# Output product of the token mixers in split one-pass products, with its weights split in eight pieces between the attention units

## The chip, the cores and the metric

The kernel runs on one core of one Trainium2 chip. The metric is the device time of one execution in microseconds, as the median of three runs. The engines meant below: TensorE (PE in the rows; PEld are its weight loads), VectorE (DVE), ScalarE (ACT), SyncE, which issues most transfers (SP).

## What is computed

A decoder trunk of two layers on 256 tokens of width 1024, in float32. Each layer adds a token mixer and then a channel mixer (dense in layer 0, top 2 of 8 experts in layer 1). The change is in the last line of the token mixer:

```python
def token_mixer(h, w_in, ..., w_out):
    proj = h @ w_in
    ...
    o_a = nsa_mixer(q, k_c, v_c, k_s, v_s, k_w, v_w, gl, cmp_pe, cmp_w1, cmp_w2)   # 512 columns
    o_b = conformer_conv(conv_in, conv_w, conv_b, conv_ln_g, conv_ln_b, conv_pw)   # 256 columns
    o_c = retention(rq, rk, rv, rg, ret_gn)                                        # 256 columns
    return jnp.concatenate([o_a, o_b, o_c], axis=-1) @ w_out                       # (256, 1024) @ (1024, 1024)

for l in range(DEPTH):
    h = rmsnorm(x, ln_attn[l])
    x = x + token_mixer(h, w_in[l], ..., w_out[l])
    h = rmsnorm(x, ln_ffn[l])
    x = x + (swiglu(h, ...) if l % 2 == 0 else moe_ffn(h, ...))
```

## The kernel before

**Two kinds of product.** A product of float32 tiles (`mm` on F32) is shown in the trace as two matmul records. The second kind, `three`, splits both operands beforehand in a rounded part (type F32R) and the remainder, and adds three one-pass matmuls: rounded by rounded, rounded by remainder, remainder by rounded. The input projections and the channel mixers are made in the second way: ACT copies a piece of the weights from the ring into its rounded part (`whM`, `whU`, `whD`), DVE subtracts that from the ring for the remainder (`ringl`, `wlU`, `wlD`). The output product and the small products of the attention are of the first kind.

**The output product.** The concatenated heads stand turned in `catT`, eight chunks of 128 channels by 256 tokens. Chunks 4 and 5 come from the convolution (stage `conv_pw`), 6 and 7 from the retention (`retcat`), 0 to 3 from the attention (`attn_sum` 0 and 1, by token tile). The output is four tiles of 128 tokens by 512 columns, k = 2 i + h for token tile i and column half h, each in a PSUM bank of its own. Stage `out` k makes the four products of chunks 4 to 7, and `out_rest` k those of chunks 0 to 3. I call such four products a group. The weights of half h are one item of the ring (`WO + h`).

**The order of the work.** Nothing schedules: `MIXER` is a list of stages written out by hand, and every engine walks it and does its own part of each stage, in order, with waits on semaphores. The attention is 12 units. Unit k has `probT` k (TensorE turns the exponentials, ACT copies them out), then what `AHEAD` names, `score` k+2 (TensorE; DVE takes the maximum; ACT the exponentials), then what `BESIDE` names for k, then `pv` k (TensorE; DVE scales it out of PSUM). `BESIDE` holds the pieces of the other mixers (`hid`, `cnorm`, `retnorm`, `cscore`, `cpv`, `out`) and `TAIL` what follows the last unit, up to the addition of the result to `x` (DVE) and its turned copy (`xT`), which the channel mixer reads. `pre` 0 and 1 split the first weights of the channel mixer.

**Banks.** PSUM groups take eight banks in turn; from the first `out` on, four banks are kept for the output and the others turn over four. A group waits until the one that held its bank before is evicted.

Of the kernel before, what the change touches and what calls it, by code (L numbers as in the profile page):

```python
# [15 lines left out]
P = 128  # L16
D = 1024
T = 256
# [58 lines left out]
def conv(a, b):  # L77
# [16 lines left out]
          3: [("reto", 0), ("hid", 0), ("cnorm", 0)], 4: [("croot", 0), ("hid", 1), ("retnorm", 0)], 5: [("cnorm", 1)],  # L94
          6: [("retnorm", 1)], 7: [("cmpkv", 0), ("conv_pw", 0)],
# [4 lines left out]
TAIL = [("osum", 1), ("pre", 0), ("out_rest", 0), ("attn_sum", 1), ("pre", 1), ("out_rest", 1), ("out_rest", 2), ("xT", 0),  # L100
        ("xT", 1), ("out_rest", 3), ("xT", 2), ("xT", 3)]
# [52 lines left out]
VW, RET, CONV, QK, W1K, W1VN, WO = range(7)  # L154
LAST_READ = (None, ("rqk", 1, 0), ("kcv", 0, 0), ("ks", 0, 0), ("cmpkv", 0, 0), ("cmpkv", 0, 0),
# [105 lines left out]
def hybrid_trunk_kernel(nc, x_in, consts_in, params_in, mix_in, ffn_in, moe_in, router_in, final_in, out):  # L261
    with ExitStack() as ctx:
# [3 lines left out]
        def sem(name):  # L266
            return ctx.enter_context(nc.semaphore(name))
# [52 lines left out]
        ro = mix("ro", [P, NT, RET_HEADS, HD])  # L320
        gates = mix("gates", [P, NT, HEADS, 3])
# [22 lines left out]
        cacc = mix("cacc", [P, 2, NC, T])  # L344
# [54 lines left out]
        whM = [nc.alloc_sbuf_tensor_at(f"whM{h}", [P, KD, FC], F32R, offset=home_at[h]) for h in range(4)]  # L399
        beforeb = sb("beforeb", [P, P], BF16)  # L400
# [77 lines left out]
        s_rk = sem("s_rk")  # L478
        s_conv_in = [sem(f"s_conv_in{h}") for h in range(2)]
# [179 lines left out]
        def _(pe):  # L659
# [81 lines left out]
            def mixer(l):  # L741
                for stage, k in MIXER[l]:
# [210 lines left out]
                    elif stage == "retcat":  # L953
                        o = begin(l, stage)
                        pe.wait_ge(s_ret, l + 1)
                        for m in range(2):
                            for i in range(NT):
                                q = m * NT + i
                                last = flip(o[:, q * P:(q + 1) * P],
                                            ro[:, i, 2 * m:2 * m + 2, :].rearrange("p h d -> p (h d)"))  # L960
                        is_full(last, l, stage)
                    elif stage == "out":
                        i, h = divmod(k, 2)
                        o = begin(l, stage, k)
# [3 lines left out]
                        landed(l, WO + h)  # L968
                        w = weights(l, WO + h, 512)
                        for c in range(KD // 2, KD):  # L970
                            mm(o, catT[:, c, i * P:(i + 1) * P], w[:, c, :], c == KD // 2, False)
                    elif stage == "out_rest":
                        i, h = divmod(k, 2)
                        w = weights(l, WO + h, 512)
# [216 lines left out]
        def _(act):  # L1191
# [40 lines left out]
            def mixer(l):  # L1232
                for stage, k in MIXER[l]:
# [110 lines left out]
                    elif stage == "attn_sum":  # L1344
                        full(act, l, stage, k)
                        is_free(A(catT[:, 0:4, k * P:(k + 1) * P],
                                  bank(l, stage, k).rearrange("p (q t) -> p q t", q=4), ACT.Copy), l, stage, k)
                    elif stage in ("conv_pw", "retcat"):
                        full(act, l, stage)
                        m = 4 if stage == "conv_pw" else 6  # L1350
                        is_free(A(catT[:, m:m + 2, :], bank(l, stage).rearrange("p (q t) -> p q t", q=2), ACT.Copy),
                                l, stage)
# [220 lines left out]
        def _(dve):  # L1573
# [64 lines left out]
            def mixer(l):  # L1638
                for stage, k in MIXER[l]:
# [627 lines left out]
```

## Time and profile before

| | us |
|---|---|
| median of three runs | 1275.2 (1274.94 to 1275.55) |
| the profiled execution | 1274.92, its span 1272.9 |
| TensorE busy | 1253.7 (98%) |
| DVE busy | 996.8 (78%) |
| ACT busy | 856.6 (67%) |
| granted TensorE clock, mean | 0.997 of 2.4 GHz |

The span is what the trace covers, so all places in it are given in us from its start. Layer 0's token mixer ends near 158 us, layer 1's near 493; the experts take the rest. A busy share is a mean over stages: an engine at 67% can still be the one that is waited for at a given place.

### The profile page before, as it was taken

Reading aid. Unit: us, or ns where it says so; the run is one execution under the profiler, and the core shown is the slowest. Engines: PE = TensorE matmul, PEld = TensorE weight load, DVE = VectorE, ACT = ScalarE, POOL = GpSimd, SP = SyncE. Lnnn points to the kernel's source line nnn. Section 1 sums busy time; section 2 is a strip of 40 time slices with the busy share of each in tenths; the row PEclk is TensorE's granted clock in tenths of the full one; section 3 lists DMA queues with packets and bytes.
Section 4 is the critical chain, followed back from the end, with each engine's and each line's share of the span. In section 5 each row is a group of like instructions: output and inputs, shape, how many; then the busy total and the mean of one; then the engine's idle time right before and its main releaser. Section 6 shows DMA issues by size and latency. Waiting matters only on the chain.

```text
span 1272.9 us, 16264 instructions
## 1 busy us (share of the span) xinstructions
PE 1253.7 (98%) x6313; PEld 1015.9 (80%) x6313; DVE 996.8 (78%) x1110; ACT 856.6 (67%) x1225; POOL 31.0 (2%) x21
## 2 busy tenths in 40 slices
PE   9999999999999999999999999999999999999996
PEld 8797588888779866788888888888888888888885
DVE  4886455455569646998999989889889889889997
ACT  4335264444451544978878888878878878878885
POOL 0000000000000000010000000000000000000300
PEclk9999999999999999999999999999999999999999
DMA  9433194442521336899999999999999999999991
GB/s 370 165 143 133 71 388 175 174 184 103 198 100 71 143 132 267 340 401 372 394 369 372 390 380 374 386 371 383 389 369 381 389 372 358 396 373 351 415 370 39
DMA packets 38625, 367.62 MB, mean 289 GB/s; under 512 B 4112, under 2 KB 7312, under 8 KB 11152
## 3 DMA queue, kind: packets, MB, share of 16 engines
q1 hardware_dynamic: 35808, 356.56, 71.2%
q0 software_dynamic: 1440, 5.24, 1.1%
q10 hardware_dynamic: 1296, 4.72, 0.9%
q8 instruction: 53, 0.87, 0.3%
q14 instruction: 28, 0.23, 0.0%
HBM read 360.73 MB, written 5.77 MB: 288 GB/s over the span
## 4 chain that ended last, share of the span: by engine, by line
PE 92%; DVE 4%; ACT 2%; issue 0%; DMA 0%; DVEq 0%; ACTq 0%
PE ps L661 88%; PE ps L664 4%; ACT arena L1294 1%; DVE blocks L1674 1%; DVE wlU L1856 1%; DVE arena L1692 0%; DVE wlD L1863 0%; ACT arena L1304 0%; DMA x<-x_in 0%; ACT xn L1196 0%; ACT L1286 0%; ACT L1341 0%; DVE arena L1765 0%; DVE xn L1596 0%; DVE ringl L1635 0%
## 5 line engine op out<-in xcount | busy, mean ns | idle before, releaser
L1856 DVE TENSOR_TENSOR wlU<-ring,whU 128x2048 fp32r<-128x2048 f32 x196 | 448.8, 2290 | 57.6 <-ACT whU L1386 53.1
L1386 ACT ACTIVATE whU<-ring 128x1024 fp32r<-128x1024 f32 x396 | 417.6, 1060 | 60.8 <-PE ps L661 53.2
L661 PE MATMUL ps<-whU,hTh 128*128 128x512 f32 x880 | 352.7, 401 | 0.8 <-DVE wlU L1856 0.8
L661 PE MATMUL ps<-whU,hTl 128*128 128x512 f32 x880 | 345.0, 392 | 0.0
L661 PE MATMUL ps<-wlU,hTh 128*128 128x512 f32 x880 | 343.0, 390 | 0.0
L1863 DVE TENSOR_TENSOR wlD<-ring,whD 128x2048 fp32r<-128x2048 f32 x97 | 222.1, 2290 | 39.2 <-ACT whD L1398 39.0
L1398 ACT ACTIVATE whD<-ring 128x1024 fp32r<-128x1024 f32 x194 | 205.2, 1066 | 58.9 <-PE ps L661 52.7
L661 PEld LDWEIGHTS ps<-whU,hTl 128*128 128x128 f32 x880 | 165.1, 188 | 36.1
L661 PEld LDWEIGHTS ps<-wlU,hTh 128*128 128x128 f32 x880 | 166.0, 189 | 32.4
L661 PEld LDWEIGHTS ps<-whU,hTh 128*128 128x128 f32 x880 | 165.3, 188 | 32.7 <-DVE wlU L1856 1.0
L661 PE MATMUL ps<-whD,gTh 128*128 128x512 f32 x428 | 168.6, 394 | 0.5 <-DVE gTl L1881 0.5
L661 PE MATMUL ps<-whD,gTl 128*128 128x512 f32 x428 | 167.4, 391 | 0.0
L661 PE MATMUL ps<-wlD,gTh 128*128 128x512 f32 x428 | 166.6, 389 | 0.0
L661 PEld LDWEIGHTS ps<-whD,gTh 128*128 128x128 f32 x428 | 80.4, 188 | 19.7 <-DVE wlD L1863 3.6
L661 PEld LDWEIGHTS ps<-wlD,gTh 128*128 128x128 f32 x428 | 80.7, 189 | 16.4
L661 PEld LDWEIGHTS ps<-whD,gTl 128*128 128x128 f32 x428 | 80.3, 188 | 16.9
L1412 ACT ACTIVATE gTh<-ps 128x256 fp32r<-128x256 f32 x107 | 40.3, 386 | 54.6 <-PE ps L664 54.6
L661 PEld LDWEIGHTS ps<-arena 128*128 128x128 f32 (+1 forms) x472 | 56.6, 190 | 14.5 <-issue 12.7
L661 PE MATMUL ps<-arena 128*128 128x64 f32 (+6 forms) x472 | 65.2, 297 | 2.3 <-ACT arena L1304 2.3
L1881 DVE TENSOR_TENSOR gTl<-ps,gTh 128x256 fp32r<-128x256 f32 x107 | 44.2, 421 | 27.5 <-ACT gTh L1412 27.5
L664 PE MATMUL ps<-cst,arena 128*128 128x128 f32 x376 | 63.3, 273 | 1.2 <-DVE arena L1802 1.1
L664 PEld LDWEIGHTS ps<-cst,arena 128*128 128x128 f32 x376 | 48.2, 143 | 17.2 <-issue 3.6
(232 smaller groups left out, 1224.7 us busy)
## 6 DMA issues: line engine op xcount, KB each, us to landing
ring<-moe_in SPq DMA_DIRECT2D x88, 2048.0 KB, 8.4
ring<-moe_in SPq DMA_DIRECT2D x88, 1024.0 KB, 8.6
ring<-ffn_in SPq DMA_DIRECT2D x11, 2048.0 KB, 7.6
ring<-mix_in SPq DMA_DIRECT2D x5, 3072.0 KB, 10.8
ring<-ffn_in SPq DMA_DIRECT2D x11, 1024.0 KB, 6.9
ring<-mix_in SPq DMA_DIRECT2D x4, 2048.0 KB, 10.5
ring<-mix_in SPq DMA_DIRECT2D x2, 2176.0 KB, 8.6
ring<-mix_in SPq DMA_DIRECT2D x2, 2112.0 KB, 8.1
```

Source lines behind the costliest of these rows:

```text
L661: return nc.tensor.matmul(o, lhsT, rhs, start=first, stop=last, skip_group_check=True)
L664: return nc.tensor.transpose(o, a, ident)
L1294: last = A(prob[:, k % 3, c * keys:(c + 1) * keys], bank(l, stage, k)[:, c * keys:(c + 1) * keys], ACT.Exp, bias=nmax[:, k, c:c + 1], scal ...
L1386: A(whU[:, p, :], ring[:, f.slot(J), p * PIECE:(p + 1) * PIECE], ACT.Copy).then_inc(s_hi, 1)
L1398: A(wh_down(f, J, c), ring[:, f.slot(J), (UP + c) * PIECE:(UP + c + 1) * PIECE], ACT.Copy)\
L1412: A(g_high(f, J, i), ps[:, up_bank(f, J, i), 0:FC].rearrange("p (c t) -> p c t", c=DOWN), ACT.Copy)\
L1674: last = V.tensor_tensor(blocks[lo:lo + HD, v, hi, :, g, 0:NBLK], src[g * HD:(g + 1) * HD, v, :, hi:hi + NBLK, r], spread(pe_[lo:lo + HD, ...
L1856: V.tensor_tensor(wlU[:, w, :], raw, whU[:, w, :].bitcast(F32), ALU.subtract).then_inc(s_lo, 1)
L1863: V.tensor_tensor(wl_down(f, J), raw, high.bitcast(F32), ALU.subtract).then_inc(s_lo, 1)
L1881: V.tensor_tensor(g_low(f, J, i), ps[:, up_bank(f, J, i), 0:FC].rearrange("p (c t) -> p c t", c=DOWN), g_high(f, J, i).bitcast(F32), ALU.s ...
```

## The change

The output product goes over to the second kind. Per layer:
- A new stage `wo` q, eight per layer: ACT copies two chunks of 512 columns of the weights (128x1024) into `woh`, DVE subtracts for the remainder in `ringl`. They stand at units 4, 5, 7, 8, 9, 10, 11 and at the head of `TAIL`.
- The heads are evicted twice: ACT writes the rounded part `cath`, then DVE reads the same bank and writes the remainder `catl`. The bank comes free after DVE.
- The groups call `out_row`, three one-pass matmuls for each chunk, and wait for their pieces of the weights.
- The groups stand elsewhere: `out` 0 at unit 8, `out` 2 at unit 9, none at unit 10, `out` 1 at unit 11, `out` 3 in `TAIL`. Before they were at 8, 9, 10 and 11.
- Some tiles are laid elsewhere in memory so that the new ones fit.

```diff
-          8: [("cscore", 0), ("out", 0)], 9: [("out", 1)],
-          10: [("cprobT", 0), ("out", 2), ("cpv", 0), ("cpv", 1)],
-          11: [("out", 3), ("asum", 0), ("asum", 1), ("osum", 0), ("attn_sum", 0)]}
+          8: [("cscore", 0), ("out", 0), ("wo", 3)], 9: [("out", 2), ("wo", 4)],
+          10: [("cprobT", 0), ("wo", 5), ("cpv", 0), ("cpv", 1)],
+          11: [("out", 1), ("wo", 6), ("asum", 0), ("asum", 1), ("osum", 0), ("attn_sum", 0)]}
...
+WO_ROWS = ((0, 4), (0, 6), (0, 0), (0, 2), (1, 4), (1, 6), (1, 0), (1, 2))
...
+            def out_row(l, o, i, h, c, first, final):
+
+                if c % 2 == 0:
+                    pe.wait_ge(s_wol, len(WO_ROWS) * l + WO_ROWS.index((h, c)) + 1)
+                t = slice(i * P, (i + 1) * P)
+                low = ringl[:, mix_load(l, WO + h) % SLOTS, 512 * c:512 * (c + 1)]
+                return three(o, cath[:, c, t], catl[c // 2][:, c % 2, t], woh[l][2 * h + (c < 4)][:, c % 4, :], low, first, final)
...
                     elif stage == "out_rest":
                         i, h = divmod(k, 2)
-                        w = weights(l, WO + h, 512)
                         freed(pe, l, "attn_sum", i)
                         for c in range(KD // 2):
-                            last = mm(bank(l, "out", k), catT[:, c, i * P:(i + 1) * P], w[:, c, :], False,
-                                      c == KD // 2 - 1)
+                            last = out_row(l, bank(l, "out", k), i, h, c, False, c == KD // 2 - 1)
...
+                    elif stage == "wo":
+                        h, c = WO_ROWS[k]
+                        n = mix_load(l, WO + h)
+                        act.wait_ge(slot_full[n % SLOTS], filled(n))
+                        if k == 0:
+                            full(act, l, "kcv")
+                        elif k == 6:
+                            full(act, l, "retcat")
+                        A(wo_high(l, k), wo_rows(ring, l, k), ACT.Copy).then_inc(s_woh, 1)
...
+                    elif stage == "wo":
+                        dve.wait_ge(s_woh, len(WO_ROWS) * l + k + 1)
+                        V.tensor_tensor(wo_rows(ringl, l, k), wo_rows(ring, l, k), wo_high(l, k).bitcast(F32), ALU.subtract)\
+                            .then_inc(s_wol, 1)
+                    elif stage in ("conv_pw", "retcat"):
+                        m = 4 if stage == "conv_pw" else 6
+                        dve.wait_ge(s_cath, CATS * l + (m == 6) + 1)
+                        is_free(V.tensor_tensor(catl[m // 2][:], bank(l, stage).rearrange("p (q t) -> p q t", q=2),
+                                                cath[:, m:m + 2, :].bitcast(F32), ALU.subtract), l, stage)
```

ACT's list in units 4 to 6, before: the copy of `hid` 1 (L1307), the copy of `probT` 5 (L1304), the exponentials of score 7 (L1294), the copy of `probT` 6, then the activation of `convB` (L1341) with its table load.

```order
L1307 ACTIVATE arena<-ps 128x256
L1304 ACTIVATE arena<-ps 128x512
L1294 ACTIVATE arena<-ps,arena 128x256 x2
L1304 ACTIVATE arena<-ps 128x512
L1341 ACT_TABLE_LOAD
L1341 ACTIVATE arena<-ps,par 128x256 x2
```

The same place of the changed kernel, whose lines stand some 27 further down:

```order
L1334 ACTIVATE arena<-ps 128x256
L1388 ACTIVATE woh_74<-ring 128x1024
L1331 ACTIVATE arena<-ps 128x512
L1321 ACTIVATE arena<-ps,arena 128x256 x2
L1388 ACTIVATE woh_74<-ring 128x1024
L1331 ACTIVATE arena<-ps 128x512
L1368 ACT_TABLE_LOAD
L1368 ACTIVATE arena<-ps,par 128x256 x2
```

The two pieces (L1388) stand right ahead of the copies of `probT` 5 and 6.

DVE's list in units 7 and 8, before: the two evictions of `cmpkv`, the three instructions of `pv` 7, the maximum of score 10, and the start of `cscore` (L1737).

```order
L1727 COPY arena<-ps 128x32
L1728 TENSOR_TENSOR arena<-ps,cst 128x512
L1699 RECIPROCAL arena<-arena 128x2
L1703 TENSOR_TENSOR arena<-arena 128x2
L1706 TENSOR_TENSOR arena<-ps,arena 128x128
L1692 TENSOR_REDUCE arena<-ps 128x2
L1694 TENSOR_SCALAR arena<-arena 128x2
L1737 SCALAR_TENSOR_TENSOR arena<-ps,cst 128x64 x4
```

And in the changed kernel, where L1848 makes the remainder of two chunks of heads and L1843 that of a weight piece:

```order
L1764 COPY arena<-ps 128x32
L1765 TENSOR_TENSOR arena<-ps,cst 128x512
L1848 TENSOR_TENSOR catl_85<-ps,cath 128x512
L1843 TENSOR_TENSOR ringl<-ring,woh_75 128x1024
L1736 RECIPROCAL arena<-arena 128x2
L1740 TENSOR_TENSOR arena<-arena 128x2
L1743 TENSOR_TENSOR arena<-ps,arena 128x128
L1848 TENSOR_TENSOR catl_86<-ps,cath 128x512
L1729 TENSOR_REDUCE arena<-ps 128x2
L1731 TENSOR_SCALAR arena<-arena 128x2
L1774 SCALAR_TENSOR_TENSOR arena<-ps,cst 128x64 x4
```

Two remainders of heads (of `conv_pw` and `retcat`) and one of weights come in ahead of the maximum of score 10.

DVE's list in units 10 and 11, before: `pv` 9 and `pv` 10 (three instructions each), then `asum` 0 and 1 (L1808) and `osum` 0 (L1812).

```order
L1699 RECIPROCAL arena<-arena 128x4
L1703 TENSOR_TENSOR arena<-arena 128x4
L1706 TENSOR_TENSOR arena<-ps,arena 128x256
L1699 RECIPROCAL arena<-arena 128x2
L1703 TENSOR_TENSOR arena<-arena 128x2
L1706 TENSOR_TENSOR arena<-ps,arena 128x128
L1808 TENSOR_TENSOR arena<-arena 128x512 x2
L1812 TENSOR_TENSOR arena<-arena 128x512
```

And in the changed kernel:

```order
L1843 TENSOR_TENSOR ringl<-ring,woh_76 128x1024
L1736 RECIPROCAL arena<-arena 128x4
L1740 TENSOR_TENSOR arena<-arena 128x4
L1743 TENSOR_TENSOR arena<-ps,arena 128x256
L1843 TENSOR_TENSOR ringl<-ring,woh_76 128x1024
L1736 RECIPROCAL arena<-arena 128x2
L1740 TENSOR_TENSOR arena<-arena 128x2
L1743 TENSOR_TENSOR arena<-ps,arena 128x128
L1843 TENSOR_TENSOR ringl<-ring,woh_77 128x1024
L1861 TENSOR_TENSOR arena<-arena 128x512 x2
L1865 TENSOR_TENSOR arena<-arena 128x512
L1854 TENSOR_TENSOR catl_83<-ps,cath 128x2x128
```

The remainders of pieces 4, 5 and 6 stand ahead of `pv` 9, `pv` 10 and the sums.

## Rows read from the trace of the kernel before

**Rows 1.** The page, its first line and the busy line of TensorE.

```profile
span 1272.9 us, 16264 instructions
PE 1253.7 (98%) x6313; PEld 1015.9 (80%) x6313; DVE 996.8 (78%) x1110; ACT 856.6 (67%) x1225; POOL 31.0 (2%) x21
```

**Rows 2.** Windows: stretch, length; busy of PE, PEld, DVE, ACT, POOL; granted clock; DMA.

```profile
98.67:158.02 59.35, 57.63 (x327) 38.16 (x326) 32.34 (x77) 26.35 (x66) 0.00 (x0) 1.00 0.27 103
434.17:493.52 59.35, 57.83 (x328) 38.36 (x328) 31.40 (x77) 29.29 (x75) 0.00 (x0) 1.00 0.27 102
```

**Rows 3.** Timeline of TensorE, layer 0: start, length, instruction, count, idle before.

```profile
106.61 0.63 PE L664 MATMUL ps<-cst,arena 128*128 128x128 f32 x4 [0.53 <-DVE arena L1802]
...
114.52 1.08 PE L661 MATMUL ps<-arena 128*128 128x64 f32 x8 [0.48 <-ACT arena L1304]
...
119.28 3.70 PE L661 MATMUL ps<-ring,arena 128*128 128x512 f32 x8
...
125.07 3.60 PE L661 MATMUL ps<-ring,arena 128*128 128x512 f32 x8
128.50 1.00 PE L661 MATMUL ps<-arena 128*128 128x64 f32 x8
...
133.44 2.72 PE L661 MATMUL ps<-arena 128*128 128x512 f32 x12
...
139.87 0.60 PE L664 MATMUL ps<-cst,arena 128*128 128x128 f32 x4
...
141.16 3.70 PE L661 MATMUL ps<-ring,arena 128*128 128x512 f32 x8
...
157.62 0.63 PE L664 MATMUL ps<-cst,x 128*128 128x128 f32 x4 [0.71 <-DVE x L1820]
```

**Rows 4.** Timeline of TensorE, channel mixer: first and last of 62 matmuls.

```profile
160.17 0.39 PE L661 MATMUL ps<-whU,hTh 128*128 128x512 f32 x1
...
174.05 0.39 PE L661 MATMUL ps<-wlU,hTh 128*128 128x512 f32 x1
```

**Rows 5.** Two copies in a row (timeline), then groups by line and form.

```profile
141.00 1.99 ACT L1386 ACTIVATE whU<-ring 128x1024 fp32r<-128x1024 f32 x2
...
L1386 ACT ACTIVATE whU<-ring 128x1024 fp32r<-128x1024 f32 x396 | 417.6, 1060 | 60.8 <-PE ps L661 53.2 <-ACT ystage L1488 3.2
...
L1849 DVE TENSOR_TENSOR wlU<-ring,whU 128x1024 fp32r<-128x1024 f32 x4 | 4.8, 1223 | 4.5 <-ACT whU L1386 4.5
```

**Rows 6.** Timeline of ACT, layer 0, units 4 to 7.

```profile
103.32 0.37 ACT L1307 ACTIVATE arena<-ps 128x256 f32<-128x256 f32 x1
103.82 0.60 ACT L1304 ACTIVATE arena<-ps 128x512 f32<-128x512 f32 x1
...
107.10 0.60 ACT L1304 ACTIVATE arena<-ps 128x512 f32<-128x512 f32 x1 [0.17 <-ACT arena L1294]
...
113.78 0.60 ACT L1304 ACTIVATE arena<-ps 128x512 f32<-128x512 f32 x1 [0.17 <-ACT arena L1294]
...
117.35 0.60 ACT L1351 ACTIVATE arena<-ps 128x512 f32<-128x512 f32 x1
```

**Rows 7.** Timeline of DVE, layer 0: end of retnorm 0, and the tail.

```profile
104.32 0.17 DVE L1776 TENSOR_SCALAR arena<-arena 128x8 f32<-128x8 f32 x1
...
152.20 0.69 DVE L1820 TENSOR_TENSOR x<-ps,x 128x512 f32<-128x512 f32 x1 [1.46 <-PE ps L661]
...
157.38 0.68 DVE L1828 TENSOR_TENSOR hT<-ps,par 128x512 f32<-128x512 f32 x1
```

**Rows 8.** Timeline of SP: the issue of the second weight half; issues with median landing.

```profile
112.28 0.33 SPq L587 DMA_DIRECT2D ring<-mix_in  x1
...
ring<-mix_in SPq DMA_DIRECT2D x4, 2048.0 KB, 10.5
```

**Rows 9.** Windows of 2 us in the router, columns as in rows 2.

```profile
498.00:500.00 2.00, 2.00 (x15) 1.28 (x14) 1.86 (x11) 0.03 (x1) 0.00 (x0) 0.50 1.05 451
500.00:502.00 2.00, 1.97 (x13) 1.41 (x12) 1.96 (x6) 1.47 (x2) 0.00 (x0) 0.78 0.90 385
```

More of the change, by code:

```diff
@@ L93 @@
 BESIDE = {0: [("rets", 0)], 1: [("rets", 1)], 2: [("convT", 0)],
-          3: [("reto", 0), ("hid", 0), ("cnorm", 0)], 4: [("croot", 0), ("hid", 1), ("retnorm", 0)], 5: [("cnorm", 1)],
-          6: [("retnorm", 1)], 7: [("cmpkv", 0), ("conv_pw", 0)],
-          8: [("cscore", 0), ("out", 0)], 9: [("out", 1)],
-          10: [("cprobT", 0), ("out", 2), ("cpv", 0), ("cpv", 1)],
-          11: [("out", 3), ("asum", 0), ("asum", 1), ("osum", 0), ("attn_sum", 0)]}
-TAIL = [("osum", 1), ("pre", 0), ("out_rest", 0), ("attn_sum", 1), ("pre", 1), ("out_rest", 1), ("out_rest", 2), ("xT", 0),
-        ("xT", 1), ("out_rest", 3), ("xT", 2), ("xT", 3)]
+          3: [("reto", 0), ("hid", 0), ("cnorm", 0)], 4: [("croot", 0), ("hid", 1), ("retnorm", 0), ("wo", 0)],
+          5: [("cnorm", 1), ("wo", 1)], 6: [("retnorm", 1)], 7: [("cmpkv", 0), ("conv_pw", 0), ("wo", 2)],
+          8: [("cscore", 0), ("out", 0), ("wo", 3)], 9: [("out", 2), ("wo", 4)],
+          10: [("cprobT", 0), ("wo", 5), ("cpv", 0), ("cpv", 1)],
+          11: [("out", 1), ("wo", 6), ("asum", 0), ("asum", 1), ("osum", 0), ("attn_sum", 0)]}
+TAIL = [("wo", 7), ("osum", 1), ("out", 3), ("pre", 0), ("out_rest", 0), ("attn_sum", 1), ("pre", 1), ("out_rest", 1),
+        ("out_rest", 2), ("xT", 0), ("xT", 1), ("out_rest", 3), ("xT", 2), ("xT", 3)]
 MIXER = [OPEN[l] + HEAD + [z for k in range(len(UNITS))
@@ L320, in hybrid_trunk_kernel @@
         ro = mix("ro", [P, NT, RET_HEADS, HD])
+        cln = mix("cln", [P, NT, CONV_CH])
+        csq = mix("csq", [P, NT, CONV_CH])
+        cacc = mix("cacc", [P, 2, NC, T])
         gates = mix("gates", [P, NT, HEADS, 3])
@@ L399, in hybrid_trunk_kernel @@
         whM = [nc.alloc_sbuf_tensor_at(f"whM{h}", [P, KD, FC], F32R, offset=home_at[h]) for h in range(4)]
+        wo_at = (xn_at, hT_at, ring_at + 4 * 4096, arena_at + 4 * mix_at["rp0"])
+        woh = [[nc.alloc_sbuf_tensor_at(f"woh{l}{q}", [P, 4, 512], F32R,
+                                        offset=wo_at[q] + 4 * SLOT * (mix_load(l, WO + 1) % SLOTS) * (q == 2))
+                for q in range(4)] for l in range(DEPTH)]
+        cath = nc.alloc_sbuf_tensor_at("cath", [P, KD, T], F32R, offset=arena_at + 4 * mix_at["catT"])
+        catl = [nc.alloc_sbuf_tensor_at(f"catl{q}", [P, 2, T], F32R,
+                                        offset=arena_at + 4 * (mix_at["cln"], mix_at["csq"], mix_at["cacc"], mix_at["cacc"] + 512)[q])
+                for q in range(4)]
         beforeb = sb("beforeb", [P, P], BF16)
@@ L478, in hybrid_trunk_kernel @@
         s_rk = sem("s_rk")
+        s_woh = sem("s_woh")
+        s_wol = sem("s_wol")
+        s_cath = sem("s_cath")
         s_conv_in = [sem(f"s_conv_in{h}") for h in range(2)]
@@ L540, in piece_of, with wo_rows, wo_high @@
             return w[:, :, col:col + FC]
+        def wo_rows(buf, l, q):
+            h, c = WO_ROWS[q]
+            return buf[:, mix_load(l, WO + h) % SLOTS, 512 * c:512 * (c + 2)].rearrange("p (c n) -> p c n", c=2)
+        def wo_high(l, q):
+            h, c = WO_ROWS[q]
+            return woh[l][2 * h + (c < 4)][:, c % 4:c % 4 + 2, :]
         def half_of(i, h):
@@ L1345, in mixer @@
                         full(act, l, stage, k)
-                        is_free(A(catT[:, 0:4, k * P:(k + 1) * P],
-                                  bank(l, stage, k).rearrange("p (q t) -> p q t", q=4), ACT.Copy), l, stage, k)
+                        A(cath[:, 0:4, k * P:(k + 1) * P], bank(l, stage, k).rearrange("p (q t) -> p q t", q=4), ACT.Copy)\
+                            .then_inc(s_cath, 1)
                     elif stage in ("conv_pw", "retcat"):
@@ L1370, in mixer @@
                             act.wait_ge(s_root, NT * 3 + i + 1)
+                            full(act, l, "out", 2)
                             A(xh[:, i, :], x[:, i, :], ACT.Copy, scale=stat[:, 3, i:i + 1]).then_inc(s_xh, 1)
@@ L1803, in mixer @@
                             .then_inc(s_cln, 1)
+                    elif stage == "wo":
[7 more added lines that the diff above has]
+                                                cath[:, m:m + 2, :].bitcast(F32), ALU.subtract), l, stage)
+                    elif stage == "attn_sum":
+                        dve.wait_ge(s_cath, CATS * l + 2 + k + 1)
+                        t = slice(k * P, (k + 1) * P)
+                        for q in range(2):
+                            last = V.tensor_tensor(catl[q][:, :, t], bank(l, stage, k).rearrange("p (q t) -> p q t", q=4)
+                                                   [:, 2 * q:2 * q + 2, :], cath[:, 2 * q:2 * q + 2, t].bitcast(F32), ALU.subtract)
+                        is_free(last, l, stage, k)
                     elif stage == "asum":
```

12 lines of the change are left out of this document (4 added, 8 removed).

## The prediction, made before the changed kernel was run

> **What bounds the kernel now.** I read the page first. TensorE is busy for 1253.7 of 1272.9 us [rows 1], so only a wait that is added to its queue, or work that is taken out of it, moves the end. Then I cut out the two stretches that the change touches, from unit 4 of the attention to the first product of the channel mixer, one for each layer [rows 2]: 59.35 us each (98.67 to 158.02 and 434.17 to 493.52, 335.50 us apart), at granted clock 1.00 (2.4 GHz). TensorE works 57.6 of them, DVE 32.3, ACT 26.4. The timeline of TensorE names its only waits there: 0.53 us ahead of convB, 0.48 ahead of pv 7 and 0.71 ahead of the last xT [rows 3]. All my times are those of layer 0; layer 1 is taken as the same. DVE and ACT seem to have 27 and 33 us to spare per layer. But each runs its list in program order, so what counts is where an inserted instruction stands in that list and who waits for the one behind it.
>
> **What the change takes off TensorE.** One group of four products (half of a 128x512 tile) lasts 125.07 to 128.50, 3.43 us [rows 3]. In one-pass form it is 12 matmuls of 512 columns. Such matmuls run back to back in the first step of the channel mixer: 61 of them start between 160.17 and 174.05, one per 0.2275 us, and 12 take 2.73 us [rows 4]. So a group gains 0.70 us; with eight groups per layer that is 5.6 us, 11.2 us for both layers. A rule that promises more: the Trainium skill, page "TensorE: Matmul & The Clock Gate", section "Back-to-back issue gap", gives about 131 ns per matmul of 512 columns in a long stream. By it a group would take 1.57 us and the gain be 29.8 us. With the waits found below the time would be 1262.8. The trace disagrees, with 227.5 ns for this same form of instruction, so that rule gets no chance and I go by the trace.
>
> **What it adds elsewhere, per layer.** ACT gets eight copies 128x1024: two of them in a row take 1.99 us, one record is 1.06 [rows 5], so the next instruction can start 0.93 after one. DVE gets eight subtractions 128x1024, 1.22 us by the four records of that size [rows 5]; the next starts some 0.07 earlier, 1.15. DVE also gets the remainders of the heads: two of 128x512 (0.69 us by an addition of that size out of PSUM [rows 7], some 0.6 to the next) and two of twice 128x256 (0.7 by the same row). That is 7.4 us on ACT and 11.8 on DVE, less than both have idle. Handovers are read from the same rows: about 0.2 us from TensorE to ACT or DVE, 0.15 back and 0.04 between ACT and DVE (estimates from where a record starts against the end of the one it waits for). I walk the list in steps.
>
> **Step A, unit 4.** On ACT weight piece 0 follows the hid 1 copy (103.32, 0.37 long [rows 6]) and ends at 104.7. The copy of probT 5, at 103.82 before, waits for it until 104.55 and pv 5 on TensorE for that copy. DVE ended retnorm 0 at 104.4 [rows 7], waits for piece 0 and subtracts until 105.85, so pv 4, the maximum of score 7 and cnorm 1 come 1.4 us late. TensorE waits at convB until 108.0 instead of 106.61.
>
> **Step B, units 5 to 7.** The exponentials of score 7 are late by 1.4 and piece 1 stands behind them, so the copy of probT 6 moves from 107.10 to 109.5, 2.4 late. From 107.10 to the copy of probT 7 at 113.78 ACT has no pause over 0.2 us (two table loads, silu, two roots) [rows 6]. All of it moves by 2.35, and with it pv 7: 116.85 instead of 114.52. TensorE is now 2.35 us late.
>
> **Step C, units 7 and 8.** DVE's list here is conv_pw remainder, piece 2, pv 7, retcat remainder, maximum of score 10. The conv_pw copy of ACT comes at 119.7 (117.35 before [rows 6]), its remainder on DVE ends at 121.0, ACT ends piece 2 at 121.2, DVE its subtraction at 122.4, pv 7 (0.6) at 123.05, and the retcat remainder at 123.7. out 0 needs that remainder: it starts at 123.85, where TensorE was ready at 119.28 [rows 3] + 2.35 = 121.6, a wait of 2.2. It is 4.55 late now. out 0 and out 2 give 1.4 back: 3.15 late.
>
> **Step D, unit 10.** Before, a group stood between cprobT and cpv 0, which began at 133.44 [rows 3], and covered ACT's two copies. It is moved away, so cpv 0 waits for the copies of probT 10 and cprobT, 0.2 + 0.49 + 0.38 + 0.15 less the 0.2 of cprobT itself, 1.05, and cpv 1 some 0.2 more for DVE. At this point 3.43 has gone and 1.25 come: 1.0 late, with a group of 2.73 still owed.
>
> **Step E, unit 11.** out 1 ends at 140.1. ACT copies probT 11 at 137.7, then piece 6 until 139.2; DVE subtracts until 140.4 and only then does the sums asum 0, asum 1 (0.7 each) and osum 0 (0.69), until 142.4. attn_sum 0 starts at 142.55 instead of 139.87 [rows 3]: a wait of 2.4, and 2.7 late.
>
> **Step F, tail.** pv 11, the owed group, then out_rest 0 at 146.55 instead of 141.16, 5.4 late. Three groups give back 2.1; out_rest 2 ends 3.2 late. The fourth gains nothing: the last xT waits for an addition that DVE does after a chain of hT and hTl pieces. That chain starts with the addition of out_rest 2 (152.20, to 157.38, then xT at 157.62 [rows 3, 7]), so it moves by some 3.1 and the shorter out_rest 3 only waits longer.
>
> **Sum.** +3.1 us per layer, made of -5.6 from the products and +8.7 of waits. The channel mixer starts 3.1 later in layer 0 and runs as before. In layer 1 the router, which hangs on the same last product, moves with it. The profiled execution took 1274.92 us, the median of the three runs is 1275.2, 0.3 more; 6.2 on the median is 1281.4.
>
> **Bounds of the unknown.** No row has these subtractions in this place. If each were hidden better than I walk it, the two soft waits (2.2 in C and 2.4 in E) could halve: 2.3 per layer off, 1276.8. If each of the eight pieces costs 0.25 more in handover, it is 4 us over both layers, 1285.4. The second half of the weights is no limit: its transfer is issued at 112.28, lands some 10.5 us later [rows 8], and ACT first needs it at 132, so even 2 us later it is there.
>
> **The rivals.**
> *All hidden, faster.* The 19 us of new work per layer fall into 27 and 33 us of idle time and TensorE keeps its pace: 1275.2 - 11.2 = 1264.0. For it: those totals. Against: the idle time lies behind waits for TensorE, and steps A and B need no assumption but the order. Chance 0.04. *Half hidden:* only A, B and D bite, 3.6 per layer against 5.6: 1271.2. It decides if the retcat remainder and osum 0 come at least 2 us earlier than I have them. Chance 0.05.
> *A draw.* C and E at half, and the maximum of score 7 not held up: about 1275. Chance 0.07.
> *The clock falls too.* In the router the granted clock went to 0.50 and 0.78 in two slices of 2 us [rows 9]. That cost 1.4 us. If each of the four longer waits (C and E, twice) brought the like, it adds about 6: 1287. Against: 0.5 us waits left the clock at 1.00. Chance 0.06.
> *As walked*, 0.78.
>
> **How the numbers follow.** A measurement tells 0.2% (2.55 us) from no change. Faster is the two hidden cases, 0.09; the draw 0.07; slower the walk and the clock, 0.84. The range 1276.8 to 1286.0 holds the walk with both bounds; outside it lie the hidden cases, most of the draw and the full fall of the clock.
>
> **What the profile after would show.** Step A: TensorE waits at pv 5 for the ACT copy and about 1.5 us at convB for cnorm. B: pv 7 starts 2.3 late, ACT without pause before it. C: the first matmul of out 0 waits 2 us for DVE's retcat remainder. D: 1 us ahead of cpv 0. E: 2.4 us ahead of attn_sum 0, released by osum. Product groups of 2.73. Windows over the same stages of 62.5 us instead of 59.35. I am wrong if out 0 or attn_sum 0 start without a wait, if the one-pass matmuls run slower or faster than 0.2275, or if the later stages shift too.

## The result, and the profile after

The changed kernel takes 1289.46 us, the median of four runs (1288.19 to 1290.35). The kernel before took 1275.38 beside it. The ratio is 1.0104, 95% interval 1.0092 to 1.0116: slower, as forecast, but by 14.1 us where I had 6.2, and outside my range (1276.8 to 1286.0).

The page of the changed kernel, its first line and TensorE's busy line, as in [rows 1]:

```profile
span 1287.1 us, 16450 instructions
...
PE 1254.2 (97%) x6377; PEld 1035.6 (80%) x6377; DVE 1020.7 (79%) x1138; ACT 871.9 (68%) x1241; POOL 28.8 (2%) x21
```

The span is 14.2 us longer. TensorE's busy time is the same, though 16 groups should have given back 11.2: something gave that back again. The windows over the same stages as in [rows 2], from probT 4 to the channel mixer:

```profile
99.26:165.16 65.90, 59.10 (x358) 49.56 (x358) 44.33 (x91) 34.01 (x74) 0.00 (x0) 0.90 0.24 92
441.33:507.14 65.81, 56.53 (x358) 46.45 (x358) 43.38 (x91) 36.81 (x83) 0.00 (x0) 0.95 0.24 92
```

They last 65.90 and 65.81 us, 6.55 and 6.46 more than before, where I had said 62.5. And the granted clock, 1.00 in both before, is 0.90 and 0.95. The rest of the 14.2 lies outside: 0.6 us ahead of the first window (probT 4 starts at 99.26, not 98.67; in e9 below, whose code is the same up to there, it starts at 98.69, so this part wanders from one execution to the next), nothing in the dense layer between the windows, 0.6 after the second.

TensorE's timeline of layer 0, with the waits of steps A and C to F:

```profile
105.85 1.08 PE L684 MATMUL ps<-arena 128*128 128x64 f32 x8 [0.56 <-ACT arena L1331]
106.77 0.61 PE L687 MATMUL ps<-cst,arena 128*128 128x128 f32 x4
108.61 0.90 PE L687 MATMUL ps<-cst,arena 128*128 128x128 f32 x4 [1.24 <-DVE arena L1839]
...
115.22 0.60 PE L684 MATMUL ps<-causalb,identb 128*128 128x512 bf16 x1
...
124.33 0.47 PE L684 MATMUL ps<-woh,cath 128*128 128x512 f32 x1 [0.41 <-DVE catl L1848]
124.64 0.40 PE L684 MATMUL ps<-ringl,cath 128*128 128x512 f32 x1
...
126.96 0.40 PE L684 MATMUL ps<-woh,catl 128*128 128x512 f32 x1
...
134.79 2.79 PE L684 MATMUL ps<-arena 128*128 128x512 f32 x12 [0.90 <-ACT arena L1348]
...
143.14 1.09 PE L687 MATMUL ps<-cst,arena 128*128 128x128 f32 x4 [2.34 <-DVE arena L1865]
...
146.58 0.63 PE L684 MATMUL ps<-woh,catl 128*128 128x512 f32 x1
147.01 0.63 PE L684 MATMUL ps<-woh,cath 128*128 128x512 f32 x1
...
150.37 0.40 PE L684 MATMUL ps<-woh,cath 128*128 128x512 f32 x1
...
164.78 0.63 PE L687 MATMUL ps<-cst,x 128*128 128x128 f32 x4 [1.36 <-DVE x L1873]
```

Two things are to be compared, where the waits stand and how long the work takes. The waits stand where the walk put them. With the 0.60 that all is late, attn_sum 0 was to start at 143.15 and did at 143.14. But the lengths do not: four turns of 128x128 take 0.61 at 106.77 and 0.90 behind the wait at 108.61, and 1.09 at 143.14. One-pass matmuls follow each other every 0.232 us at 124.64 to 126.96 and every 0.43 at 146.58. The windows of 4 us at those places say why:

```profile
104.00:108.00 4.00, 2.81 (x20) 2.14 (x18) 3.66 (x10) 1.80 (x5) 0.00 (x0) 1.00 0.00 0
108.00:112.00 4.00, 3.39 (x16) 3.24 (x17) 2.22 (x5) 3.85 (x8) 0.00 (x0) 0.60 0.00 0
112.00:116.00 4.00, 4.00 (x20) 3.67 (x19) 1.95 (x5) 3.94 (x11) 0.00 (x0) 0.54 0.00 0
...
144.00:148.00 4.00, 4.00 (x16) 3.52 (x15) 3.04 (x8) 3.43 (x4) 0.00 (x0) 0.50 0.02 4
148.00:152.00 4.00, 4.00 (x16) 3.18 (x15) 2.17 (x1) 0.00 (x0) 0.00 (x0) 0.78 0.00 0
```

The clock is at its lower level (0.50, 1.2 of 2.4 GHz) behind two waits: the pair 0.56 and 1.24 ahead of convB, and 2.34 ahead of attn_sum 0. Layer 1 has the same waits, but keeps its clock at convB:

```profile
450.68 0.63 PE L687 MATMUL ps<-cst,arena 128*128 128x128 f32 x4 [1.24 <-DVE arena L1839]
...
466.40 0.47 PE L684 MATMUL ps<-woh,cath 128*128 128x512 f32 x1 [2.10 <-DVE catl L1848]
...
470.82 1.00 PE L684 MATMUL ps<-arena 128*128 128x64 f32 x8
...
486.76 0.63 PE L687 MATMUL ps<-cst,arena 128*128 128x128 f32 x4 [2.34 <-DVE arena L1865]
```

There it falls behind out 0's wait, so that its group takes 4.42 us (466.40 to 470.82) instead of the 2.7 of the walk, and again behind attn_sum 0.

**What each fall cost.** In layer 0 the stages from convB to score 9 take 6.61 us (108.61 to 115.22) instead of the 3.53 of e8's rows below, 3.1 more. Yet out 0 starts on time, at 124.33 (walk: 123.85 + 0.60). The delay took the place of waits: that of pv 7, which is 1.09 in e8 and gone here, and that of out 0, of which 0.41 is left. The second fall has no such wait behind it. attn_sum 0 to out_rest 0 takes 7.23 instead of the 4.0 of my walk: +3.2. In layer 1 the two falls cost 1.7 each. So my theory after the result: per layer the walk's 3.1, as predicted, and 3.2 to 3.4 of clock. The rival: the waits and transfers between engines are longer than walked, and the clock is a symptom of TensorE idling more.

### The profile page after: what moved, and what is told of

Its sections match the earlier page's. It is cut to its first block, busy times and chain, and to the rows that moved or that the text cites. A ratio compares the mean times of both kernels' runs of the same rounds, so it can differ in the third digit from the quotient of the medians.

```text
span 1287.1 us, 16450 instructions
## 1 busy us (share of the span) xinstructions
PE 1254.2 (97%) x6377; PEld 1035.6 (80%) x6377; DVE 1020.7 (79%) x1138; ACT 871.9 (68%) x1241; POOL 28.8 (2%) x21
## 4 chain that ended last, share of the span: by engine, by line
PE 89%; DVE 6%; ACT 3%; issue 1%; DMA 0%; DVEq 0%; SPq 0%; ACTq 0%
PE ps L684 86%; PE ps L687 3%; ACT arena L1321 1%; DVE wlU L1909 1%; DVE blocks L1711 1%; DVE arena L1729 1%; ACT woh L1388 0%; DMA par<-params_in 0%; DVE ringl L1843 0%; DVE wlD L1916 0%; ACT arena L1331 0%; DVE x L1873 0%; ACT whU L1423 0%; DVE arena L1743 0%; DVE arena L1861 0%
## 5 line engine op out<-in xcount | busy, mean ns | idle before, releaser
L684 PE MATMUL ps<-arena 128*128 128x64 f32 (+6 forms) x472 | 68.3, 305 | 5.3 <-ACT arena L1331 3.5
L684 PEld LDWEIGHTS ps<-arena 128*128 128x128 f32 (+1 forms) x472 | 59.3, 198 | 15.8 <-issue 12.7
```

Of the source, the lines that this page charges most:

```text
L684: return nc.tensor.matmul(o, lhsT, rhs, start=first, stop=last, skip_group_check=True)
```

## The experiments

All ratios are to the kernel before, run beside each on the same chip (its medians: 1275.4 to 1276.3).

**e1 and e5: hold the clock, change nothing else.** `keep_busy(o, n)` issues n matmuls on constants of 128x256 (fillers), whose result the next product overwrites; the kernel before has it too, in other places, the router among them. In e1 they stand ahead of four waits, at convB (10) and out 0 (14), shown here, and likewise at pv 7 (8) and attn_sum 0 (18):

```diff
                     elif stage == "convB":
                         o = begin(l, stage)
+                        keep_busy(o, 10)
                         pe.wait_ge(s_cln, l + 1)
...
                         o = begin(l, stage, k)
                         if k == 0:
+                            keep_busy(o, 14)
                             freed(pe, l, "retcat")
```

> The changed kernel with empty bf16 matmuls (128x256, into the bank that is about to be written) put ahead of four of TensorE's waits in each layer: 10 ahead of the wait of convB, 8 ahead of pv 7, 14 ahead of out 0, 18 ahead of attn_sum 0. They only fill time in which TensorE waited. Theory (the clock): the waits themselves cost 6.3 us by my walk, the rest of the 14.1 us is the granted clock that falls behind them, so with the waits filled the clock stays at 1.00 there and the time is 1281 to 1283. Rival (the waits and the slower work are all from the other engines being late): filling changes nothing, 1289, or more, as the fillers delay. The granted clock of the stretches 98 to 166 us tells it apart.

Measured: 1288.05 us (1286.69 to 1288.29), ratio 1.0086 [1.0069, 1.0102]. Neither theory's time. The falls at convB and attn_sum 0 are gone, but at out 0 the clock fell in both layers (0.57 at 124 to 128 us, 0.71 at 464 to 468). The trace shows a flaw of mine: out 0's bank is the one that DVE evicts with the retcat remainder, so `begin` itself waits and the fillers stood behind the wait (2.06 us, released by L1854), adding 2.4 and 2.8 us to it. So e1 decides nothing for that place; e5 puts 16 fillers there, into the bank of `pv` 8, the stage that follows, which is free by then:

```diff
                         i, h = divmod(k, 2)
+                        if k == 0:
+                            keep_busy(begin(l, "pv", 8), 16)
                         o = begin(l, stage, k)
```

> The first filler kernel again with the fillers of out 0 in another place: in it they stood behind the wait for the bank of retcat, so they did not fill the wait of 2.06 us but followed it, 2.7 us long. Here 16 of them write into the bank of pv 8 ahead of that wait; the others stay (10 at convB, 8 at pv 7, 18 at attn_sum 0). Theory (the clock is what the walk lacked): granted clock 1.00 in all of both mixers, time 1282 (1281 to 1284). Rival (something else costs 8 us): 1287 or more with the clock at 1.00.

Measured: 1283.38 us (1282.84 to 1283.74), ratio 1.0059 [1.0044, 1.0075]. The windows over the same stages of e5:

```profile
98.81:161.52 62.71, 59.08 (x410) 48.79 (x410) 44.30 (x91) 34.02 (x74) 0.00 (x0) 1.00 0.26 97
437.81:500.43 62.62, 59.37 (x411) 48.88 (x410) 43.30 (x91) 36.82 (x83) 0.00 (x0) 1.00 0.25 96
```

With the clock at 1.00 the windows are 62.71 and 62.62: the 62.5 of the prediction. DVE and ACT do what they did in the changed kernel. This separates the two parts: some 6 us of the 14.1 are the clock (1289.46 to 1283.38), and the walk of waits and products is right to 0.2 us per layer. TensorE at `out` 0 and behind `out` 2 in e5:

```profile
123.88 0.47 PE L684 MATMUL ps<-woh,cath 128*128 128x512 f32 x1 [0.25 <-DVE catl L1854]
...
131.78 1.00 PE L684 MATMUL ps<-arena 128*128 128x64 f32 x8
```

The fillers delay nothing: `out` 0 starts 25.07 us after probT 4 (98.81 to 123.88), as it does in the changed kernel (99.26 to 124.33). The rival would have left windows of 65.8.

**e9 and e10: one fall at a time.** e9 keeps only the 18 fillers at attn_sum 0, e10 only those at convB (10) and pv 7 (8).

> The changed kernel with one addition: 18 matmuls on constants, whose result nobody reads, ahead of attn_sum 0 in both layers, in the 2.34 us in which TensorE waits there for osum. All else is as in the changed kernel. Theory (the clock's fall behind this wait is paid in full, because no later wait takes it up): attn_sum 0 to out_rest 0 is 3.2 us shorter in layer 0 and 1.7 in layer 1, so 4.9 in all, 1284.6 us; the granted clock is 1.00 from 140 to 152 us, and still falls behind convB in layer 0 and at out 0 in layer 1. Rival (the fall belongs to the stretch, not to the wait, and comes a little later all the same): 1288 to 1290, with the clock down somewhere between 145 and 160.

> The changed kernel with fillers only at its early waits: 10 matmuls on constants ahead of convB and 8 ahead of pv 7, in both layers. Theory (a fall ahead of out 0 is taken up by out 0's wait on the retcat remainder, since DVE sets when that comes): in layer 0 the clock stays at 1.00 from 104 to 120 us, TensorE comes to out 0 some 3 us earlier and waits there some 2 us instead of 0.41, and out 0's first product starts within 0.3 us of where it did. Nothing is gained: 1289, and up to 1291 if the clock then falls behind that longer wait, as it does in layer 1. Rival (each fall costs what it takes away, wherever it is): 3.1 less, 1286.3.

e9: 1286.34 us (1285.15 to 1287.94), ratio 1.0081 [1.0068, 1.0095], 3.1 faster than the changed kernel, not 4.9. e10: 1289.68 (1289.55 to 1290.58), ratio 1.011 [1.0095, 1.0126]: nothing gained, as its theory said. TensorE in e10:

```profile
106.90 1.26 PE L684 MATMUL ps<-warm 128*128 128x256 bf16 x10
108.22 0.66 PE L687 MATMUL ps<-cst,arena 128*128 128x128 f32 x4
...
124.04 0.47 PE L684 MATMUL ps<-woh,cath 128*128 128x512 f32 x1 [2.11 <-DVE catl L1850]
...
125.25 0.63 PE L684 MATMUL ps<-ringl,cath 128*128 128x512 f32 x1
```

The early fall is gone, and TensorE waits 2.11 at out 0 instead of 0.41. `out` 0 starts 25.10 us after probT 4 (98.94 to 124.04), as against 25.07 in the changed kernel: the early fall cost nothing at this point. Then the clock falls behind that longer wait, and out 0's group takes 4.42. That the whole window comes out the same as well (98.94 to 164.90, 65.96 us, as against 65.90) is in part luck: the fall behind attn_sum 0 was shorter here (5.72 us from attn_sum 0 to out_rest 0, as against 7.23) and gave back what out 0 had lost. So a fall ahead of a wait for another engine is free, and taking it away can bring on the next one. e9 shows the other half:

```profile
108.05 0.63 PE L687 MATMUL ps<-cst,arena 128*128 128x128 f32 x4 [1.24 <-DVE arena L1841]
...
123.77 0.77 PE L684 MATMUL ps<-woh,cath 128*128 128x512 f32 x1 [2.10 <-DVE catl L1850]
124.33 0.63 PE L684 MATMUL ps<-ringl,cath 128*128 128x512 f32 x1
...
141.58 2.14 PE L684 MATMUL ps<-warm 128*128 128x256 bf16 x18
143.99 0.66 PE L687 MATMUL ps<-cst,arena 128*128 128x128 f32 x4 [0.27 <-DVE arena L1867]
```

The fall behind attn_sum 0 is gone. But in layer 0 convB, with the same 1.24 us wait and the same work ahead, kept its clock this time (0.63, not 0.90), and out 0 lost it. That is the miss of 1.7: my expectation took the other falls as fixed. The same code has the fall now behind one wait, now behind the next, and the loss at one place is now 1.6, now 3.1.

**e8: pieces 0 and 1 alone, in the kernel before.** It tests steps A and B without the rest.

```diff
-          4: [("croot", 0), ("hid", 1), ("retnorm", 0)], 5: [("cnorm", 1)],
+          4: [("croot", 0), ("hid", 1), ("retnorm", 0), ("wo", 0)], 5: [("cnorm", 1), ("wo", 1)],
```

> The kernel before with only two of the eight weight pieces split at units 4 and 5, where the change has its first two; nothing reads them, products and order stay. It tests steps A and B alone. Theory: convB 1.4 us late, pv 7 2.35 late, and no later place gives it back, as in my walk: 2.35 per layer, 1281.0 with the clock at 1.00, and if the clock falls behind convB's wait, as in the changed kernel in layer 0, 1 to 4 more, up to 1285. Rival (the later idle time takes it in): 1277.

Measured: 1281.46 us (1279.61 to 1281.67), ratio 1.0039 [1.0023, 1.0054]. Two of eight pieces, with none of the products changed, cost 5 to 6 us (2.9 to 6.9 by the interval). TensorE in e8:

```profile
105.59 1.08 PE L664 MATMUL ps<-arena 128*128 128x64 f32 x8 [0.56 <-ACT arena L1307]
...
108.35 0.63 PE L667 MATMUL ps<-cst,arena 128*128 128x128 f32 x4 [1.24 <-DVE arena L1812]
...
111.88 0.38 PE L664 MATMUL ps<-causalb,identb 128*128 128x512 bf16 x1
...
117.15 1.08 PE L664 MATMUL ps<-arena 128*128 128x64 f32 x8 [1.09 <-ACT arena L1307]
```

With 0.33 us that e8 is late at its first window, pv 7 is 2.3 late against [rows 3]: step B's 2.35. The waits are those of the changed kernel to the hundredth, and the clock stayed at 1.00.

**e3: the order alone.** The kernel before with only the new places of the groups.

```diff
-          8: [("cscore", 0), ("out", 0)], 9: [("out", 1)],
-          10: [("cprobT", 0), ("out", 2), ("cpv", 0), ("cpv", 1)],
-          11: [("out", 3), ("asum", 0),
+          8: [("cscore", 0), ("out", 0)], 9: [("out", 2)],
+          10: [("cprobT", 0), ("cpv", 0), ("cpv", 1)],
+          11: [("out", 1), ("asum", 0),
```

> The kernel before with only the new places of the groups (out 0 at unit 8, out 2 at unit 9, none at unit 10, out 1 at unit 11, out 3 after the last unit), its product and weights untouched. Theory: only cpv 0 loses its cover, a wait of 1.0 us per layer, minus nothing: 1277.2, and the clock stays at 1.00 as no wait is over 1.1 us. Rival (the moved groups alone let the clock fall or start later waits): 1280 or more.

Measured: 1278.19 us (1277.28 to 1279.32), ratio 1.0015 [1.0006, 1.0025], 1.9 us more than before, where the theory had 2.0. TensorE ahead of cpv 0:

```profile
131.93 2.79 PE L661 MATMUL ps<-arena 128*128 128x512 f32 x12 [0.90 <-ACT arena L1321]
```

Step D stands: the group that was moved away had covered 0.90 us of ACT (1.05 walked).

**e7: the old product in the new surroundings.** All of the splits are done, but each chunk is multiplied once as float32, rounded heads by the remainder of the weights; the other parts of the sum are left out.

```diff
-                return three(o, cath[:, c, t], catl[c // 2][:, c % 2, t], woh[l][2 * h + (c < 4)][:, c % 4, :], low, first, final)
+                return mm(o, cath[:, c, t].bitcast(F32), low.bitcast(F32), first, final)
```

> The changed kernel with all its splits and order, only the product itself as before (one float32 product of the rounded heads with the remainder half of the weights in the place of three one-pass ones: part of the computation is left out). It prices the gain alone. By the walk the end of the mixer comes 4.0 us later per layer than in the changed kernel (5.6 less what waits give back), so 1297 if the clock falls as there; if the longer groups keep the clock up, 1290 to 1292. Rival (one-pass products gain nothing here, as TensorE only waits more): 1289.

Measured: 1295.87 us (1295.12 to 1298.62), ratio 1.0163 [1.0148, 1.0179]. So in these surroundings the one-pass products are worth 6 to 7 us (6.4 by the medians, 7.5 by the two ratios), not 11.2. TensorE at `out` 0 and at attn_sum 0 shows where a part of it goes:

```profile
123.83 5.37 PE L684 MATMUL ps<-ringl,cath 128*128 128x512 f32 x8 [2.10 <-DVE catl L1848]
...
145.61 0.63 PE L687 MATMUL ps<-cst,arena 128*128 128x128 f32 x4 [1.66 <-DVE arena L1865]
```

With the longer out 1 this wait is 1.66 instead of 2.34: the gain of out 1 only lengthens a wait, as that of out_rest 3 does (0.7 us each, 2.8 in both layers). And the clock stays at 1.00 behind 1.66, so the falls that attn_sum 0 brings in the changed kernel are part of the products' price. It falls behind out 0's wait in both layers (5.37 us for a group of 3.5 to 3.7), so e7 isn't free of the clock either, and the 6 to 7 us are a net of both.

**e2: take the subtractions' length away.** DVE subtracts 8 of each 512 columns, and the products read the rounded weights in the place of the remainder: the weights' remainder is left out, the number and form of the matmuls stay.

```diff
-                low = ringl[:, mix_load(l, WO + h) % SLOTS, 512 * c:512 * (c + 1)]
+                low = woh[l][2 * h + (c < 4)][:, c % 4, :]
...
-                        V.tensor_tensor(wo_rows(ringl, l, k), wo_rows(ring, l, k), wo_high(l, k).bitcast(F32), ALU.subtract)\
+                        c = slice(0, 8)
+                        V.tensor_tensor(wo_rows(ringl, l, k)[:, :, c], wo_rows(ring, l, k)[:, :, c],
+                                        wo_high(l, k)[:, :, c].bitcast(F32), ALU.subtract)\
```

> The changed kernel, where DVE subtracts only 8 of the 512 columns of each weight chunk (0.15 us instead of 1.22 per piece) and the products read the rounded weights in the place of the remainder: the remainder of the weights is left out, number and form of the matmuls stay. Theory (DVE's eight subtractions hold up the heads of the other chains in order): by the walk the waits at convB, out 0 and attn_sum 0 shrink from 1.5, 2.1 and 2.5 to 0.4, 1.3 and 1.5 us, the mixers end 3.1 us earlier each, and with shorter waits the clock falls less: 1275 if it does not fall, up to 1280 if it does. Rival (ACT's copies alone do it): within 2 us of the changed kernel, 1287 to 1290.

Measured: 1279.88 us (1278.61 to 1281.34), ratio 1.0029 [1.0019, 1.0038]. Its waits in layer 0 (producer, us, number, longest):

```profile
PE ps L684 <- ACT arena L1331: 2.3, 4, 1.1
...
PE ps L684 <- DVE catl L1850: 1.4, 1, 1.4
PE ps L687 <- DVE arena L1867: 1.3, 1, 1.3
PE ps L684 <- ACT arena L1348: 0.9, 1, 0.9
PE ps L687 <- DVE arena L1839: 0.2, 1, 0.2
```

DVE's length is worth 9.6 us: 1.0 each at convB (1.24 to 0.2) and attn_sum 0, 0.7 at out 0, per layer, and a part of the clock (it still went to 0.65 at 124 to 128 us). ACT's waits (2.3 and 0.9) are untouched. Even so the kernel isn't faster than before: the copies, the remainders of the heads, the moved group and what is left of the clock's falls cost all that the products gain.

**e4 and e6: other places, same instructions.** In e4 ACT's and DVE's halves of a piece are stages of their own, put behind what TensorE waits for, and the product groups and sums change places too.

```diff
+          4: [("woh", 0), ("croot", 0), ("hid", 1), ("retnorm", 0)], 5: [("wol", 0), ("cnorm", 1)],
+          6: [("woh", 1), ("retnorm", 1)], 7: [("wol", 1), ("cmpkv", 0), ("conv_pw", 0)],
+          8: [("cscore", 0), ("woh", 2)], 9: [("wol", 2), ("woh", 3), ("wol", 3), ("out", 0)],
+          10: [("cprobT", 0), ("out", 2), ("woh", 4), ("woh", 5), ("wol", 4), ("wol", 5), ("cpv", 0), ("cpv", 1)],
+          11: [("asum", 0), ("asum", 1), ("osum", 0), ("out", 1), ("woh", 6), ("wol", 6), ("attn_sum", 0)]}
```

> The changed kernel with the same instructions in another order: the eight ACT copies and the eight DVE subtractions are stages of their own, put where each engine waited for TensorE before (copies 0 to 7 at units 4, 6, 8, 9, 10, 10, 11 and behind the last; subtractions 0 to 7 at units 5, 7, 9, 9, 10, 10, 11 and behind out 3), out 0 at unit 9, out 2 at unit 10 between cprobT and cpv 0, out 1 at unit 11 behind the sums, out 3 after the last unit. Theory (the loss is the places, not the work): by the same walk no wait of TensorE is over 1.3 us, the mixers end 4.2 us earlier than in the kernel before, the clock holds, 1267. Rival (19 us of added work per layer on ACT and DVE cannot be hidden, or the clock falls from any added wait): 1276 or more.

Measured: 1271.54 us (1268.36 to 1275.05), ratio 0.9951 [0.9934, 0.9969]: faster than before, though not by what I had (1267). Its four executions lie further apart than those of any other kernel here, and the time goes with the mean granted clock: 1268.36 and 1269.78 at 0.996, 1273.3 at 0.993, 1275.05 at 0.990. The trace is of the last one. Windows of e4 behind convB in layer 0, in layer 1, and in the router:

```profile
108.00:112.00 4.00, 4.00 (x17) 3.73 (x18) 0.29 (x1) 3.71 (x7) 0.00 (x0) 0.50 0.00 0
...
444.00:448.00 4.00, 4.00 (x17) 3.64 (x17) 0.87 (x3) 3.50 (x8) 0.00 (x0) 0.50 0.00 0
492.00:496.00 4.00, 4.00 (x28) 4.00 (x27) 1.78 (x2) 1.57 (x3) 0.00 (x0) 0.70 0.99 418
```

A wait of 0.9 at convB is left, and the clock fell behind it in both layers. e6 is e4 with 5 fillers at pv 5, 8 at convB, 2 at pv 7 and 4 each at two of the xT.

> The reordered kernel with fillers: 5 ahead of the wait of pv 5, 8 at convB, 2 at pv 7, and 4 at the second and fourth xT. In the reordered kernel the granted clock still fell to 0.50 from 107.9 to 114.6, behind waits of 0.62 and 0.91 us, and again in layer 1 at 442 to 450 and in the router. Theory (the clock again): with the waits filled the clock holds in the attention and the time goes from 1271.5 to 1267 (1265.5 to 1268.5). Rival: the fall comes from narrow work (64 to 128 columns), not the waits, fillers do not hold it, 1271 to 1273.

Measured: 1269.01 us (1268.78 to 1270.65), ratio 0.9948 [0.9934, 0.9961], the fastest median, though its interval doesn't tell it from e4, and above the 1265.5 to 1268.5 of its theory. Its windows over the stages are 57.08 and 55.56 us, against 59.35 before:

```profile
98.97:156.05 57.08, 56.65 (x381) 47.31 (x381) 43.97 (x91) 33.92 (x74) 0.00 (x0) 0.97 0.28 106
432.27:487.83 55.56, 55.55 (x384) 46.40 (x384) 43.09 (x92) 36.72 (x83) 0.00 (x0) 1.00 0.29 110
...
120.00:124.00 4.00, 4.00 (x28) 3.55 (x27) 3.35 (x14) 2.59 (x7) 0.00 (x0) 0.71 1.01 418
```

The last line is a fall without a wait: from 103 to 128 us no wait of TensorE is listed in e6, it is busy for all of the 4.00 us here and for all but 0.02 of the 16 us ahead of it, and yet the clock falls, among matmuls of which most are 32 to 256 columns wide. The router shows the same in the kernel before:

```profile
493.38 3.64 PE L661 MATMUL ps<-router,hTr 128*128 128x8 f32 x32
496.87 2.60 PE L661 MATMUL ps<-warm 128*128 128x256 bf16 x14
```

The last wait ahead of it is 0.51 us long, then TensorE turns out matmuls of 8 columns and fillers without a pause, and the clock goes to 0.50 [rows 9]. So waits are not the only thing that brings a fall.

**e11: more fillers.**

> The version with other places for groups and pieces and with fillers (best so far, 1269.0), with 2 and 3 fillers more ahead of pv 8 and pv 9 and 5 each ahead of the router's first and third set of logits. Theory (what is left in it of the falls, 1 to 2 us at 120 to 126 us and 1.5 to 2 us in the router, comes from a run of narrow matmuls, and wider work among them holds the clock): 1266.5, with the clock at 1.00 at 120 to 128 us and in the router. Rival (the fillers are paid, some 0.2 us each where there is no wait, and the clock falls all the same): 1270 to 1272.

Measured: 1271.22 us (1270.16 to 1271.5), ratio 0.9962 [0.9948, 0.9976]. Half of the theory came true: the mixers' clock is 1.00 throughout, at 120 to 128 us too, where e6 had lost it, as the theory has it for wider work among the narrow matmuls (one trace of each). In the router it still went to 0.87 and 0.70 (488 to 496 us). For the time the rival holds: past the real waits, fillers buy nothing that can be measured.

## Why the prediction was wrong

The sign and steps A to F were right; the failed step is the **Sum**, which has no term for the clock. I had it as the rival "The clock falls too" (1287) and gave it 0.06.

- **Product gain** (0.70 per group said): 0.66. In e5 the stretch from `out` 0 to the end of `out` 2 takes 7.90 us (123.88 to 131.78), before it took 9.22 (119.28 to 128.50 [rows 3]). The matmuls follow each other every 0.232 us, not 0.2275, which is only part of it. By this rate eight groups give 5.3 per layer, not 5.6.
- **Step A**: pv 5 waits 0.56, convB 1.24 (about 1.5 said).
- **Step B**: 2.3 late (e8; 2.35 said).
- **Step C**: 2.10 in layer 1 and 2.11 in e10 (2.2 said). In layer 0 of the changed kernel the early fall had taken it up.
- **Step D**: 0.90 ahead of cpv 0 (1.05 said); of the 0.2 more for cpv 1 the rows show 0.1 (134.79 to 137.43, 2.64 us, as against 2.55 before).
- **Step E**: 2.34, released by osum (2.4 said).
- **Step F**: the last xT waits 1.36, 0.65 longer, so out_rest 3 gains nothing, as said.
- **Sum** without the clock: the walk gave windows of 62.5; e5, with the clock held, has 62.71 and 62.62. The 0.3 that the products' gain is short of is the larger part of the difference; the waits come out within 0.3 of the walk in all. e5's 1283.4 is inside the range, 2.0 above the forecast. Of those 2.0 the windows hold 0.4, the stretches outside them 0.8 (0.14 ahead, 0.14 in the dense layer, 0.5 behind, where the router has its own fall). The last 0.8 lies outside the span (1282.84 for 1280.3, 0.5 more than before) and between that execution and the medians.
- **The missing term**: some 6 us (e5 against the changed kernel). In the trace, against the same stretches of e5, it is 3.1 + 1.6 + 1.6 = 6.3 for three of four falls (7.23 and 5.69 from attn_sum 0 to out_rest 0, where e5 has 4.14; 4.42 for out 0's group in layer 1, where e5 has 2.86), the fourth absorbed.

Where did I go wrong in judging that rival? I argued from "0.5 us waits left the clock at 1.00", which bears on waits like those before. The walk itself had made waits of 2.2 and 2.4 us, and the longest on TensorE in the trace before is 1.1: no row of it could say that such waits leave the clock alone, so the 0.06 had no row behind it. The router's fall [rows 9], from which I took the price, isn't even a case of a wait, as the rows above show; it came without one. That the price fits (about 6 in all) is luck in part: of the four falls that I counted, at C and E in each layer, three came, one of them at 3.1, twice the 1.5 that I had for each, and the fourth, at C in layer 0, was replaced by one behind convB's wait, which cost nothing. The section "What's actually happening" of the page that the prediction cites, the Trainium skill, "TensorE: Matmul & The Clock Gate", goes the same way: it says that the low clock is the default and that activity releases it, judged by how busy the array has been recently. The trace agrees, with 0.50 behind 2.34 us of idle. The section also says that the monitor runs freely and isn't tied to the program's start; that would explain why the fall sits at convB in one execution and at out 0 in e9, but no run here shows the monitor itself.

**All hidden**, **Half hidden** and **A draw** needed the soft waits of C and E gone or halved; they came at 2.10 and 2.34, nearly full length.

## What to carry to other kernels

When a walk of the queues ends with new waits on TensorE of a microsecond or more, add a clock term to the sum: here 1.6 to 3.1 us for each wait of 2.1 to 2.3, unless a wait for another engine follows soon and takes it up. The totals of idle time did not tell what an inserted copy costs: two of eight pieces cost 5 to 6 us here because they stood ahead of what TensorE waited for, and all the instructions of the change, a few places later (e4), made the kernel 0.5% faster than before. A filler held the clock here where it stood ahead of the wait, that of its own bank included (e5), and not where it stood behind (e1).

## What the runs showed of the hardware

- The clock fell behind idle times as short as 0.56 and 1.24 us less than 2 us apart, and behind 0.62 and 0.9 in e4, each among matmuls of 32 to 256 columns. Behind the same 0.56 and 1.24 in layer 1, in e8 and in e9 it did not. Every wait of 2.06 to 2.35 us at out 0 and attn_sum 0 brought one, in the changed kernel, e1, e7, e9 and e10. What decides for the shorter ones stays open.
- It also fell with no wait at all: to 0.71 in e6 (120 to 124 us) and to 0.50 in the router of the kernel before, behind 32 records of matmuls of 8 columns and the fillers that follow them.
- At the lower level one-pass matmuls of 512 columns follow each other every 0.43 us instead of 0.23, and four turns of 128x128 take 1.06 to 1.09 instead of 0.61.
- The lower clock was paid only where TensorE set the end. 3.1 us of it in layer 0 cost nothing up to out 0 (e10: 25.10 us without the fall, 25.07 with it).
- e7's wait of 1.66 ahead of attn_sum 0 left the clock at 1.00; so did e2's of 1.3 there. But e2's of 1.35 at out 0 brought a fall (0.65 and, in layer 1, 0.67).
